# Networks with the turns of both token tiles in one group, dilated pairs whose values follow the next pair's scores, and rows of 1024 bytes for the transposed activations

## What is computed

```python
for i in range(DEPTH):
    a = rmsnorm(h, norm_mix_pre[i])
    m = nsa_mixer(a, ...) if i % 2 == 0 else dilated_mixer(a, ...)
    h = h + rmsnorm(m, norm_mix_post[i])
    f = swiglu(rmsnorm(h, norm_ffn_pre[i]), ffn_w_gu[i], ffn_w_down[i])
    h = h + rmsnorm(f, norm_ffn_post[i])

def swiglu(h, w_gu, w_down):
    gu = h @ w_gu
    g, u = gu[..., :D_FF], gu[..., D_FF:]
    return (jax.nn.silu(g) * u) @ w_down

def dilated_mixer(a, cos, sin, w_in, w_o):
    for gi, (window, dil) in enumerate(((128, 1), (512, 4), (2048, 16))):
        # q, k (rotated) and v of pattern gi; banded attention within each residue of dil
    alpha = softmax over the patterns of their log-sum-exp
    return (sum over patterns of alpha * o) @ w_o
```

## Time and profile before

| | |
|---|---|
| time, median of 3 runs | 832.33 us (832.21 to 832.71) |
| profiled execution, its time | 832.52 us |
| its span | 830.8 us |
| granted TensorE clock, mean | 0.997 of full speed |
| PE busy | 818.2 us (98%), 4452 matmul records |
| PEld busy | 649.5 us (78%) |
| DVE busy | 513.4 us (62%) |
| ACT busy | 456.7 us (55%) |
| loaded from HBM | 134.64 MB, 165 GB/s over the span |

### The profile page before, as it was taken

One profiled execution on the slowest core, in us unless ns is written; L12 is line 12 of the kernel. 1 busy time (PEld: TensorE's weight loads), 2 busy tenths in 40 slices (PEclk: granted clock), 3 DMA queues, 4 the chain that ended last, 5 costly groups with the idle time before them and its releaser, 6 DMA issues.

```text
span 830.8 us, 11698 instructions
## 1 busy us (share of the span) xinstructions
PE 818.2 (98%) x4452; PEld 649.5 (78%) x4452; DVE 513.4 (62%) x1075; ACT 456.7 (55%) x879; POOL 36.5 (4%) x95
## 2 busy tenths in 40 slices
PE   8999999999999999999999999999999999999996
PEld 7877666788888888888877878777878888888885
DVE  5856869786545555586465565565568765555544
ACT  7846877764444344475565555555657544344431
POOL 1000004800000000000000000000000000000000
PEclk9999999999999999999999999999999999999998
DMA  9955311165664466568544435352524665456501
GB/s 320 315 196 183 96 52 52 49 228 171 217 217 159 151 199 214 161 215 274 172 159 144 161 116 189 106 199 102 160 95 155 192 212 177 152 186 217 204 1 50
DMA packets 108904, 137.49 MB, mean 165 GB/s; under 512 B 6273, under 2 KB 92337, under 8 KB 108721
## 3 DMA queue, kind: packets, MB, share of 16 engines
q1 hardware_dynamic: 107760, 132.53, 48.3%
q0 software_dynamic: 992, 4.19, 1.4%
q10 hardware_dynamic: 96, 0.02, 0.0%
HBM read 134.64 MB, written 2.10 MB: 165 GB/s over the span
## 4 chain that ended last, share of the span: by engine, by line
PE 94%; DVE 4%; ACT 1%; issue 1%; POOL 0%; ACTq 0%; POOLq 0%; DVEq 0%
PE ps L1685 84%; PE ps L1694 7%; PE ps L1935 1%; PE ps L1908 1%; DVE w_lo L1138 1%; PE ps L1746 0%; ACT xt_hi L646 0%; PE ps L1947 0%; DVE xt_lo L1186 0%; DVE probs L1331 0%; ACT junk L658 0%; DVE h L1456 0%; DVE h L1462 0%; DVE tmp L1460 0%; DVE probs L1357 0%
## 5 line engine op out<-in xcount | busy, mean ns | idle before, releaser
L1138 DVE TENSOR_TENSOR w_lo<-w_raw,w_hi 128x1024 fp32r<-128x1024 f32 x240 | 287.7, 1223 | 93.7 <-ACT w_hi L637 91.2
L1685 PE MATMUL ps<-w_hi,xt_hi 128*128 128x512 f32 x760 | 311.6, 410 | 1.2 <-DVE w_lo L1138 0.8
L1685 PE MATMUL ps<-w_lo,xt_hi 128*128 128x512 f32 x760 | 299.4, 394 | 0.0
L1685 PE MATMUL ps<-w_hi,xt_lo 128*128 128x512 f32 x760 | 298.9, 393 | 0.0
L637 ACT ACTIVATE w_hi<-w_raw 128x1024 fp32r<-128x1024 f32 x240 | 246.2, 1059 | 0.0
L1685 PEld LDWEIGHTS ps<-w_hi,xt_hi 128*128 128x128 f32 x760 | 143.8, 189 | 37.5 <-issue 9.2
L1685 PEld LDWEIGHTS ps<-w_hi,xt_lo 128*128 128x128 f32 x760 | 143.3, 189 | 32.3
L1685 PEld LDWEIGHTS ps<-w_lo,xt_hi 128*128 128x128 f32 x760 | 143.9, 189 | 25.5
L909 ACT ACTIVATE st_hi<-ps 128x256 fp32r<-128x256 f32 x40 | 15.4, 385 | 119.4 <-PE ps L1694 119.4
L1474 DVE TENSOR_TENSOR st_lo<-ps,st_hi 128x256 fp32r<-128x256 f32 x40 | 17.0, 425 | 78.1 <-ACT st_hi L909 77.9
L1685 PE MATMUL ps<-w_hi,st_hi 128*128 128x512 f32 x160 | 63.2, 395 | 0.0
(11 more groups left out here) (244 smaller groups left out, 802.2 us busy)
## 6 DMA issues: line engine op xcount, KB each, us to landing
w_raw<-in_ffn_w_gu SPq DMA_DIRECT2D x88, 512.0 KB, 5.0
w_raw<-in_dil_w_in SPq DMA_DIRECT2D x72, 512.0 KB, 4.6
w_raw<-in_ffn_w_down SPq DMA_DIRECT2D x44, 512.0 KB, 4.7
w_raw<-in_nsa_w_in SPq DMA_DIRECT2D x20, 512.0 KB, 7.6
w_raw<-in_nsa_w_o SPq DMA_DIRECT2D x8, 512.0 KB, 4.9
w_raw<-in_dil_w_o SPq DMA_DIRECT2D x8, 512.0 KB, 4.3
w_k<-in_nsa_cmp_wk SPq DMA_DIRECT2D x2, 1024.0 KB, 7.9
w_raw<-in_nsa_cmp_wv SPq DMA_DIRECT2D x2, 1024.0 KB, 11.1
```

The source lines that it names most:

```text
L1138: dve.tensor_tensor(w_lo[:, n.slot, c:c + 1024], w_raw[:, n.slot, c:c + 1024], w_hi[:, n.slot, c:c + 1024].bitcast(F32), ALU.subtract)\
L1685: ins = pe.matmul(o, s, m, start=start, stop=stop, **kw)
```

## The change

1. `xt_hi` and `xt_lo` become [128, 8, 256], with rows of 1024 bytes, at the same addresses. The dilated layer's projections go on with rows of 1088 bytes, through the names `xd_hi` and `xd_lo` over the same memory.
2. In `step` of the network the turn of (j - 1, 1) moves from the middle of gu(j, 0) to the middle of gu(j, 1), right ahead of the turn of (j, 0). The copies on ScalarE and VectorE move with it, and TensorE waits for `hs_ready` of (j - 1, 1) before gu(j, 1).
3. In the dilated layer, where pairs are three slots apart and t < 3, the values come in phase 3, behind the scores of the next pair; else in phase 4, as before. The turn of the second head's probabilities (phase 3) stands ahead of the scores of its slot. ScalarE copies it earlier in its order: in an even slot ahead of the evacuation of the last projection, in an odd one ahead of the copies of the turned queries and keys.

```diff
+def value_phase(g, t):
+    return 3 if t < 3 and pair_start(g, 1) - pair_start(g, 0) == 3 else 4
+
+def values_at(s):
+    return [(g, t) for g in range(DIL_G - 1) for t in range(4) if pair_start(g, t) + value_phase(g, t) == s]
...
-        xt_hi = sb("xt_hi", [P, KT, XT_PITCH], F32R)
-        xt_lo = sb("xt_lo", [P, KT, XT_PITCH], F32R)
+        at_xt = [zone(KT * XT_PITCH * 4) for k in range(2)]
+        xt_hi, xt_lo = (sb(f"xt_{k}", [P, KT, S], F32R, at=at) for k, at in zip(("hi", "lo"), at_xt))
+        xd_hi, xd_lo = (sb(f"xd_{k}", [P, KT, XT_PITCH], F32R, at=at) for k, at in zip(("hi", "lo"), at_xt))
...
 # ScalarE, ffn; VectorE alike
                     split(nx)
-                    ht_out(j - 1, 1)
                     split(nx + 1, (0,))
                     silu_step(j, 0)
                     split(nx + 1, (1,))
                     split(nx + 2, (0,))
+                    ht_out(j - 1, 1)
                     ht_out(j, 0)
                     split(nx + 2, (1,))
                     silu_step(j, 1)
...
 # ScalarE, dilated layer
+            def dil_odd_out(s):
+                for g, t in pairs_at(s, 3):
+                    dil_pt_out(pair_units(g, t)[1])
...
-                for g, t in pairs_at(s, 3):
-                    dil_pt_out(pair_units(g, t)[1])
...
             for e in range(4, LAST_E):
                 k = 2 * TILES[e].chunk + TILES[e].m
+                dil_odd_out(2 * e)
                 dil_evac(TILES[e - 1])
                 split(n + k, (0,))
                 dil_attend(2 * e)
+                dil_odd_out(2 * e + 1)
                 if e == 4:
                     split(n + k, (1,))
                 dil_turn_out(TILES[e - 1])
...
 # TensorE, ffn
                 def step(j, pc):
-                    gu(j, 0, pc, mid=lambda: ht_turn(j - 1, 1))
+                    def turns():
+                        ht_turn(j - 1, 1)
+                        ht_turn(j, 0)
+
+                    gu(j, 0, pc)
                     down(j - 1, 0, pc + 2)
-                    gu(j, 1, pc, mid=lambda: ht_turn(j, 0))
+                    pe.wait_ge(hs_ready[layer], ffn_order(j - 1, 1) + 1)
+                    gu(j, 1, pc, mid=turns)
                     down(j - 1, 1, pc + 2)
...
 # TensorE, dil_attend
                 for g, t in pairs_at(s, 2):
                     dil_turn_probs(pair_units(g, t)[0])
-                for g, t in pairs_at(s, 4):
-                    dil_pv(g, t)
+                for g, t in pairs_at(s, 3):
+                    dil_turn_probs(pair_units(g, t)[1])
+                for g, t in values_at(s):
+                    if value_phase(g, t) == 4:
+                        dil_pv(g, t)
                 for g, t in pairs_at(s, 0):
                     if t == 0:
                         pe.wait_ge(turn_out[1], 6 * (g + 1))
                     dil_scores(g, t)
-                for g, t in pairs_at(s, 3):
-                    dil_turn_probs(pair_units(g, t)[1])
+                for g, t in values_at(s):
+                    if value_phase(g, t) == 3:
+                        dil_pv(g, t)
```

More of the change, by code:

```diff
@@ L644, in xt_out @@
                     kt = 4 * half + k
-                    src, dst = xt_views(b, m, half, kt, xt_hi)
+                    src, dst = xt_views(b, m, half, kt, xd_hi if b == 2 else xt_hi)
                     ins = act.activation(dst, src, ACT.Copy, scale=g_t[:, 8 * gain + kt:8 * gain + kt + 1])
@@ L1183, in xt_lo_out @@
                     kt = 4 * half + k
-                    src, dst = xt_views(b, m, half, kt, xt_lo)
-                    _, hi = xt_views(b, m, half, kt, xt_hi)
+                    src, dst = xt_views(b, m, half, kt, xd_lo if b == 2 else xt_lo)
+                    _, hi = xt_views(b, m, half, kt, xd_hi if b == 2 else xt_hi)
                     ins = dve.scalar_tensor_tensor(dst, src, g_t[:, 8 * gain + kt:8 * gain + kt + 1],
@@ L1527, in ffn @@
                     dve.wait_ge(xt_ready[2], 2)
-                    dve.tensor_copy(xt_hi[:, :, S:S + 2], xt_hi[:, :, 0:2])
-                    dve.tensor_copy(xt_lo[:, :, S:S + 2], xt_lo[:, :, 0:2]).then_inc(xt_padded, 1)
+                    dve.tensor_copy(xd_hi[:, :, S:S + 2], xd_hi[:, :, 0:2])
+                    dve.tensor_copy(xd_lo[:, :, S:S + 2], xd_lo[:, :, 0:2]).then_inc(xt_padded, 1)
             norm_nsa(15)
@@ L1705, in three, with gemm @@
                 return mm(o, s_lo, m_hi, False, stop)
-            def gemm(b, m, pc, first, last, done=None, mid=None, need=None, cols=None, half_done=None):
+            def gemm(b, m, pc, first, last, done=None, mid=None, need=None, cols=None, half_done=None,
+                     hi=xt_hi, lo=xt_lo):
                 for half in range(2):
@@ L1722, in gemm @@
                         at = cols or slice(m * P, (m + 1) * P)
-                        ins = three(bank(b), xt_hi[:, kt, at], xt_lo[:, kt, at],
+                        ins = three(bank(b), hi[:, kt, at], lo[:, kt, at],
                                     w_hi[:, p.slot, c:c + 512], w_lo[:, p.slot, c:c + 512],
@@ L2232, in dil_gemm @@
                      cols={QK: None, V01: slice(x.m, S, 2), V2: slice(x.m + 2, S + 2, 2)}[x.kind],
-                     need=need, mid=mid)
+                     need=need, mid=mid, hi=xd_hi, lo=xd_lo)
             def dil_turn(x):
```

## The result

The changed kernel takes 825.86 us (median of 4 runs, 825.44 to 826.34) against 832.27 us: the ratio is 0.9923, 95% interval 0.9905 to 0.9940, 6.4 us or 0.8% faster. 825.7 was forecast, with a range of 824.3 to 829.5. The profiled execution has a span of 824.1 us where the one before had 830.8.

What follows compares the result with a forecast made beforehand. TensorE, busy for 98% of the span, was taken as the bound, through its start-to-start matmul distance. Gains of 5.1 + 0.6 + 0.9 = 6.6 us took 832.52 to 825.9, or 825.7 as median; range 824.3 to 829.5.

Steps and rivals of the forecast that it cites:

- The rows in the networks: Network half steps: 1024-byte rows bring matmuls to 226.7 ns; 6.0 us to gain, less 0.9 lost at turns: 5.1 us.
- what an interruption leaves behind: Matmuls behind a group of turns: time still lost to upset rhythm, taken as 0.03 us a group, about 15 per network.
- The attention layer: Projections reading xt_hi: even rows gain 0.35 us in whole ones, 0.2 in threes; 0.6 with the dilated layer's output.
- The output projection of the dilated layer: Its 24 matmuls reading xt_hi: a small gain, counted within the attention layer's 0.6 us (0 to 1.1).
- The turns by themselves: Network steps: same 88 turns, 0.11 us each whatever their group, so regrouping is worth 0 by itself.
- The dilated pairs: Dilated stage, head groups 0 and 2: six merged groups, each 2.52 becoming 2.37 us, give 0.9 us (0.9 to 1.3).
- turns directly ahead of scores: Dilated merged groups: cost of three turns before scores, in no trace row; between 0.27 and 0.33 us, 0.33 taken.
- The covers and the signs: Slack hiding moved copies: 1.7 us in networks, about 0.3 for dilated values; dilated projections' matmuls stay at 231 ns.
- the *moving* start: Stationary rows kt start 1088 x kt bytes further on; taken as cause of 231.4 ns a matmul instead of 226.7.
- even rows could be the worst case: Rival: all loads and moving rows starting at the same place slow 1416 matmuls by 5 ns, +7 us; 838.5; chance 0.04.
- The rival of the 512 bytes between `xt_hi` and `xt_lo`: Switching between the two costs some 2.5 ns on 1400 matmuls: 3.5 us less gain, 829.2; chance 0.11.
- the two rivals that end at 829: Rows 512 apart disturb (829.2, chance 0.11); a new wait for ScalarE's copies in the networks (828.9, chance 0.06).

Runs made afterwards that it cites:

- e1: The kernel before with only the 1024-byte rows of xt_hi and xt_lo (dilated projections keep 1088): 827.01 us, ratio 0.9936.
- e2: The kernel before with only the networks' turns of both token tiles in one group, rows of 1088 bytes kept: 832.36 us, ratio 1.0001.
- e3: The kernel before with only the new order of the dilated pairs: 831.28 us, ratio 0.9987.
- e4: The changed kernel with xt_hi and xt_lo both moved by 64 bytes, rows still 1024 apart: 833.59 us, 1.0013 of before.
- e12: The changed kernel with dilated projections' rows 1280 bytes apart for kt = 1 to 7 and row kt = 0 in other memory: 824.83 us, ratio 0.9909.
- e9: The changed kernel with xt_hi and xt_lo both moved by 128 bytes: 832.33 us, ratio 1.0001.
- e11: The changed kernel with xt_hi and xt_lo both moved by 192 bytes: 827.86 us, ratio 0.9946.
- e5: The changed kernel with every tensor in SBUF moved by 64 bytes, so none changes place against another: 825.89 us, ratio 0.9923.
- e6: The changed kernel with the dilated projections' rows 1032 bytes apart instead of 1088: 826.68 us.
- e7: The changed kernel with the dilated projections' rows 1040 bytes apart instead of 1088: 826.63 us.

## Why the prediction was right, and where it was not

**The terms.** The rows in the networks were put at 5.1 us: e1 has 2.29 + 2.24 = 4.53 for them, and 0.32 more comes with the turns, which the prediction had counted there as interruptions saved; together 4.85. The term that was a little mis-sized is what an interruption leaves behind: 0.03 was taken, the one step shown above has 0.05, and the missing 6.0 - 4.85 = 1.15 us make 0.04 for each of the 28 groups of turns that the two networks still have. The attention layer was put at 0.6 and gave 0.53. The output projection of the dilated layer gave 0.01. The turns by themselves were put at 0: e2 has 0.0. The dilated pairs were put at 0.9: e3 and the whole change have 0.93, and the merged group costs 2.37 as in the sum. In that term the step that no row had shown, turns directly ahead of scores, was decided by an argument between 0.27 and 0.33. The measured sum fits 0.33, if values cost as much behind scores as ahead of them; the reason given, that scores lose more at their entry, was not tested.

**The covers and the signs.** All held. The dilated projections, which keep their pitch, still run at 231 to 232 ns. ScalarE's and VectorE's copies in the networks end 1.6 us before they are needed (1.7 was the estimate), the copy of the second probabilities 0.4 us before (0.3).

**The mechanism.** The time was forecast well, the reason only in part. The prediction read from the earlier trace rows that the start of the rows matters, and that held. But it took the *moving* start for the cause: a rhythm that every uneven row upsets anew. That is only part of it. e4 shows that rows 1024 bytes apart can take 233.3 ns as steadily as the change's rows take 226.7; what decides there is the place of the rows within 256 bytes. A change of place does upset some eight or ten matmuls, as the prediction said (the down projection in e4, row kt = 4 before), but even rows help only at a good place. The forecast came out because the change kept the start of `xt_hi`, which is that of `st_hi` and the good one of four. The prediction had seen that start at 226.7 ns and counted on it, so its number did not hang on the reason; yet by its reason any start would have done, and that it had the good one in hand was luck. The rival "even rows could be the worst case" named the danger and was rightly given a small chance, since kt = 0 had been seen at 226.7; but its reason (all starts alike is bad) was wrong as well, and at the three other places the kernel's time against before is from -4.4 to +1.3 us instead of the +6 it stated. The rival of the 512 bytes between `xt_hi` and `xt_lo` fell too: 512 is two periods.

**The range.** It was made wide enough to take in the two rivals that end at 829, neither of which happened.

## What to carry to other kernels

Where a long row of matmuls bounds a kernel, measure the distance from start to start, not the length of the records, and compare operands that do the same work from other addresses: the rows alone took 0.6% off this kernel (e1), and cost only a change of where a tensor lies. For tiles like these, rows a multiple of 256 bytes apart with the base tried in steps of 64 are worth the test, and the test matters: the right pitch at the wrong base can be slower than uneven rows (e4). Try each kind of read by itself, for the best place of one was not that of another (value tiles in e12, the 256-column product). Put small work on TensorE (turns, scores, values) into fewer groups where that saves a passage into scores or values and back: six merged groups gave 0.93 us even among uneven rows (e3). Regrouping turns alone gave nothing there (e2) and 0.3 us on even rows.

## What the runs showed of the hardware

- The start-to-start distance of 128x512 fp32r matmuls, each with its own 128x128 load, at the full granted clock depends on where the stationary tile starts within 256 bytes: 226.7, 233.3, 232.9 and 229.2 ns at 0, 64, 128 and 192 bytes from the good place (rows of the changed kernel, e4, e9, e11). Moving everything by 64 bytes changes nothing (e5). Against what the start counts is not shown; the other operand is the likeliest.
- In a product of 256 columns the start of the moving operand counts as well: 120 ns with the changed kernel's rows, 113.5 with the activations moved by 192 bytes (e11).
- A change from a slow place to the good one leaves about eight distances uneven (e4, 2.74 us for 12 matmuls where 2.72 are due).
- Offsets of 8 to 56 and of 16 to 112 bytes from the good place are no better than 64 to 448 (e6, e7).
- A stationary tile read in steps of two elements takes about 233 ns even from the good place (e12, 4.20 us for 18), and 231.6 from 8 or 12 bytes behind it.
- A group of turns leaves the matmuls behind it uneven for some ten of them: 0.05 us in the step shown, 0.02 for each group saved between e1 and the changed kernel.
- Going from the projections into scores or values and back costs about 0.2 us more than passing from values to scores directly (1.24 + 1.01 - 2.04). Three turns directly ahead of scores cost 2.37 - 2.04 = 0.33 us, as much as alone, if values cost the same behind scores as ahead of them.
